# ScalarE takes a second turned map and a second scaling from VectorE in a decoder layer's attention rounds

## What is computed

```python
def masked_softmax(s, mask):
    s = jnp.where(mask, s, NEG_INF)
    e = jnp.where(mask, jnp.exp(s - jnp.max(s, axis=-1, keepdims=True)), 0.0)
    return e / jnp.maximum(jnp.sum(e, axis=-1, keepdims=True), 1e-30)

# differential attention, prompt
p = masked_softmax(s, kpos[None, :] <= qpos[:, None])
a = p[:, :, 0] - lam * p[:, :, 1]
return jnp.einsum('bhqk,bkhv->bqhv', a.astype(v.dtype), v)

# sparse attention: every branch is a masked softmax times its values, then
o_nsa = jnp.sum(o_branches * g_n[..., None], axis=2)
```

## Time and profile before

| | us |
|---|---|
| median of 3 runs | 759.29 (755.44 to 765.13) |
| the profiled execution | 756.94 |
| its span | 755.3 |

### The profile page before, as it was taken

How to read it: one execution, slowest core, us unless ns; L and a number is a source line. 1 busy time by engine, 2 the same in 40 slices (tenths; PEclk the granted TensorE clock), 3 DMA queues, 4 the chain that set the end, 5 groups by cost and what they waited for, 6 DMA issues and landing times.

```text
span 755.3 us, 14050 instructions
## 1 busy us (share of the span) xinstructions
PE 696.8 (92%) x4419; PEld 327.8 (43%) x4419; DVE 488.7 (65%) x976; ACT 205.7 (27%) x530; POOL 105.0 (14%) x198
## 2 busy tenths in 40 slices
PE   6979999999998979999999998968897888999996
PEld 2445545445453535444534643425343352343542
DVE  5366774863865547998597539657769657544373
ACT  3031012112021004322231226524555334333200
POOL 0000000000001001010003556612647100000000
PEclk9999999999999989999999999999999988999999
DMA  8997987998999979999868369978999969985721
GB/s 313 378 330 221 331 263 244 329 368 260 340 379 362 397 261 344 401 320 356 336 209 295 99 194 326 327 243 300 256 318 316 316 205 387 349 268 180 278 114 57
DMA packets 131683, 218.46 MB, mean 289 GB/s; under 512 B 17617, under 2 KB 55738, under 8 KB 130394
## 3 DMA queue, kind: packets, MB, share of 16 engines
q1 hardware_dynamic: 103752, 185.76, 71.6%
q10 hardware_dynamic: 20402, 17.02, 7.3%
q0 software_dynamic: 7456, 14.80, 6.0%
HBM read 211.64 MB, written 10.04 MB: 294 GB/s over the span
## 4 chain that ended last, share of the span: by engine, by line
PE 57%; issue 17%; DVE 8%; DMA 6%; ACTq 4%; POOLq 4%; SPq 2%; POOL 2%; ACT 1%; DVEq 0%
PE banks L690 17%; PE banks L648 9%; PE banks L703 6%; PE banks L1071 4%; ACTq L457 3%; PE banks L789 3%; PE banks L1192 3%; POOLq L476 2%; PE banks L968 2%; DMA ring<-in_dk_cache 1%; PE banks L638 1%; DMA proj<-in_cmp_cache 1%; DMA xn<-in_win_v 1%; POOL ring L480 1%; PE banks L985 1%
## 5 line engine op out<-in xcount | busy, mean ns | idle before, releaser
L690 PE MATMUL banks<-ring,xt 128*128 128x512 f32 (+1 forms) x320 | 130.3, 560 | 0.0
L1445 ACT ACTIVATE wide<-banks,att 128x384 f32<-128x384 f32 (+3 forms) x128 | 66.3, 523 | 121.5 <-DVE att L1947 120.3
L690 PEld LDWEIGHTS banks<-ring,xt 128*128 128x128 f32 x320 | 59.4, 191 | 66.7 <-issue 63.1
L480 POOL DMA_DIRECT2D ring<-in_sel_cache x143 | 75.2, 526 | 45.8 <-issue 40.0
L789 PE MATMUL banks<-ring,small 128*32 128x512 f32 x512 | 70.6, 632 | 2.7 <-DVE xt L1990 2.7
L703 PE MATMUL banks<-ring,small 128*32 128x512 f32 x512 | 62.8, 608 | 3.4 <-DMA ring<-in_dk_cache 3.3
L1946 DVE TENSOR_TENSOR banks<-banks,consts 128x256 f32<-128x256 f32 x64 | 27.4, 428 | 45.9 <-PE banks L968 45.5
L690 PE MATMUL banks<-xt,ring 128*128 128x512 f32 x128 | 56.7, 595 | 0.0
L968 PE MATMUL banks<-proj 64*128 64x384 f32 (+7 forms) x256 | 52.5, 487 | 2.9 <-ACT wide L1445 2.9
L1254 ACT ACTIVATE proj<-banks 128x512 f32<-128x512 f32 (+1 forms) x26 | 14.6, 566 | 147.9 <-PE banks L690 114.7
L1947 DVE TENSOR_REDUCE att<-banks 128x2 f32<-128x768 f32 (+3 forms) x64 | 52.8, 825 | 2.2
(11 more groups left out here) (379 smaller groups left out, 924.4 us busy)
## 6 DMA issues: line engine op xcount, KB each, us to landing
ring<-in_dk_cache SPq DMA_DIRECT2D x256, 256.0 KB, 5.1
ring<-in_dv_cache SPq DMA_DIRECT2D x256, 256.0 KB, 5.2
proj<-in_cmp_cache SPq DMA_DIRECT2D x120, 128.0 KB, 5.4
proj<-in_cmp_cache ACTq DMA_DIRECT2D x104, 128.0 KB, 5.7
ring<-in_w_in SPq DMA_DIRECT2D x6, 2048.0 KB, 13.7
ring<-in_sel_cache POOLq DMA_DIRECT2D x143, 32.0 KB, 5.5
ring<-in_w_out SPq DMA_DIRECT2D x2, 2048.0 KB, 9.3
out_s_win<-in_win_nat SPq DMA_DIRECT2D x1, 4088.0 KB
```

The costliest lines, as they stand in the source:

```text
L480: eng.dma_start(sel_kv[64 * (n % 2):64 * (n % 2) + 64, q % 8, n // 2, :], src["sel_cache"][bass.ds(at, 1), :, :].rearrange("o k n -> (o k) ...
L690: last = mm(banks[:, 3 + n % 2, 0:width(c)], of, by, start=k == 0, stop=k == KC - 1)
L1445: last = A(e_slot(j, c)[:, 0:n], banks[:, 2 * (j % 2) + c, 0:n], ACT.Exp, bias=row_max[:, j % 4, c:c + 1], accum_out=row_sum[:, j % 4, c:c ...
```

## The change

ScalarE's `keep_b0` also copies kind 1 out of bank 5, so it now runs in all four kinds and `keep_b1` on VectorE only in kinds 2 and 3. In the large pair's rounds of kinds 2 and 3 (`by_scalar`) `scale_first` scales both maps, one instruction after the other, and VectorE's L1964 is gone there. In the small pair it stays. No transfer is added or moved. The counts that TensorE waits for follow: bank 5 is free for kind 2 when ScalarE has copied kind 1.

```diff
         def copies_before(j, b):
-            return 3 * (j // 4) + ((0, 1, 1, 2), (0, 0, 1, 2))[b][j % 4]
+            return (4, 2)[b] * (j // 4) + ((0, 1, 2, 3), (0, 0, 0, 1))[b][j % 4]
+        def by_scalar(j):
+            return j % 4 >= 2 and duo(j)[1] == 1
+        def scaled_rounds(j):
+            return sum(not by_scalar(i) for i in range(j + 1))
...
             def turn(j):
                 r, tp, t, kind, n = duo(j)
-                pe.wait_ge(s("scaled"), j + 1)
+                if not by_scalar(j):
+                    pe.wait_ge(s("scaled"), scaled_rounds(j))
...
                     bank = kind if kind < 2 else c
-                    if copies_before(j, bank):
-                        pe.wait_ge(s(f"b{bank}_kept"), copies_before(j, bank))
+                    if kind != 1 and copies_before(j, 0):
+                        pe.wait_ge(s("b0_kept"), copies_before(j, 0) - (1 if kind == 2 and c == 0 else 0))
+                    if bank == 1 and copies_before(j, 1):
+                        pe.wait_ge(s("b1_kept"), copies_before(j, 1))
...
             def values(m):
-                pe.wait_ge(s("b0_kept"), 6 * m + 6)
-                pe.wait_ge(s("b1_kept"), 6 * m + 6)
+                pe.wait_ge(s("b0_kept"), 8 * m + 8)
+                pe.wait_ge(s("b1_kept"), 4 * m + 4)
...
             def scale_first(j):
-                e0 = e_slot(j, 0)[:, 0:n]
-                A(e0, e0, ACT.Copy, scale=row_sum[:, j % 4, 0:1]).then_inc(s("scaled_first"), 1)
+                for c in range(2 if by_scalar(j) else 1):
+                    e = e_slot(j, c)[:, 0:n]
+                    last = A(e, e, ACT.Copy, scale=row_sum[:, j % 4, c:c + 1])
+                last.then_inc(s("scaled_first"), 1)
             def keep_b0(j):
-                to = p_turned_d(0) if kind == 0 else p_turned_n[:, 2 * (kind - 2), :, :]
-                A(to[...], banks[:, 4, 0:n]..., ACT.Copy).then_inc(s("b0_kept"), 1)
+                to = p_turned_d(kind) if kind < 2 else p_turned_n[:, 2 * (kind - 2), :, :]
+                A(to[...], banks[:, 4 + (kind == 1), 0:n]..., ACT.Copy).then_inc(s("b0_kept"), 1)
...
-                if 3 <= j < DUOS + 3 and j % 4 != 0:
+                if 3 <= j < DUOS + 3:
                     keep_b0(j - 3)
...
             def scale(j):
-                    dve.wait_ge(s("weighed"), nsa_rounds(j))
-                    V.tensor_scalar(e1, e1, sums[:, 1:2], None, ALU.mult).then_inc(s("scaled"), 1)
+                    if not by_scalar(j):
+                        dve.wait_ge(s("weighed"), nsa_rounds(j))
+                        V.tensor_scalar(e1, e1, sums[:, 1:2], None, ALU.mult).then_inc(s("scaled"), 1)
             def keep_b1(j):
-                to = p_turned_d(1) if kind == 1 else p_turned_n[:, 2 * (kind - 2) + 1, :, :]
+                to = p_turned_n[:, 2 * (kind - 2) + 1, :, :]
...
-                if 3 <= j < DUOS + 3 and j % 4 != 3:
+                if 3 <= j < DUOS + 3 and (j - 3) % 4 >= 2:
                     keep_b1(j - 3)
```

More of the change, by code:

```diff
@@ L1459, in keep_b0 @@
                 act.wait_ge(s("turned_p"), turns_done(j, 0))
-                to = p_turned_d(0) if kind == 0 else p_turned_n[:, 2 * (kind - 2), :, :]
-                A(to[:, 0:t + 1, P * (t % 2):P * (t % 2) + P], banks[:, 4, 0:n].rearrange("p (k n) -> p k n", n=P),
+                to = p_turned_d(kind) if kind < 2 else p_turned_n[:, 2 * (kind - 2), :, :]
+                A(to[:, 0:t + 1, P * (t % 2):P * (t % 2) + P], banks[:, 4 + (kind == 1), 0:n].rearrange("p (k n) -> p k n", n=P),
                   ACT.Copy).then_inc(s("b0_kept"), 1)
```

## The result

| | before | after |
|---|---|---|
| median, us | 758.26 (752.26 to 765.13, 20 executions) | 760.55 (756.41 to 765.48, 20 executions) |
| profiled execution (span) | 756.94 (755.3) | 761.08 (759.1) |

The ratio is 1.0061, with a 95% interval of 1.0038 to 1.0084: 0.6% slower, and within the 2% that counts as the same. It counts fast executions alone (none over 1.5% above the fastest of its kernel), while the two medians in the table count all and stand at 1.0030. The forecast was 760.9 us, a ratio of 1.0021 to its own base of 759.29.

What follows compares the result with a forecast made beforehand. Bounds took turns: GpSimd's block loads, the selection's ping-pong, those loads again, a mixture, finally TensorE. Terms +0.5 + 0 + 0.35 - 0.2 + 1.0 = +1.65, say +1.6, on 759.29 gave 760.9 us; own range 758.5 to 763, with rivals 755.5 to 766.

Steps and rivals of the forecast that it cites:

- Step 1: Rounds 0 to 12: about 4 us off VectorE come out before a 6.21 us transfer wait at the first gate: 0.0.
- rival C: Waits for ScalarE's copy bite everywhere: 16 turns of kind 2 hold TensorE 0.7 us each, +11, 771 us; chance 0.05.
- Step 2: Rounds 13 to 17, first selection: second scaling and copy on ScalarE delay it, +0.5 us, bounds 0 and +1.2.
- Step 3: Rounds 18 to 36: the stretch still ends with GpSimd's load series, 0.0 us, bounds -0.39 and +1.
- Step 4: Round 41: TensorE's turn of kind 2 waits for ScalarE's copy, delaying value step and second selection, +0.35 us.
- Step 5: Round 44: one copy goes from in front of VectorE's `keep_n(4)`, for which `out_sums(0)` waited 1.54 us: -0.2 us.
- Step 6: Rounds 53 and 61: TensorE waits for ScalarE's copy behind the exponentials, +0.5 us each; bounds for the pair 0 and +1.5.
- rival B: TensorE's clock: earlier arrival and longer idling at both gates bring one to three more half-clock stretches, 762.5 to 766; chance 0.2.
- Rivals A and D: First: GpSimd's series gets shorter, 756.9, chance 0.13. Second: VectorE was the pace, all 14.7 us come out, 744.6, chance 0.03.

Runs made afterwards that it cites:

- the repeat: The changed kernel run once more, unedited, against the kernel before: 759.98 us, ratio 1.0061 (1.0027 to 1.0095).

## Why the prediction was right

The time was right, 760.9 against 760.55, and four of the six steps were; but that the two numbers lie so close is in part luck. The forecast was +1.6 us on a base of 759.29, the median of three executions, and the median of twenty is 758.26. Against that base the change costs 2.3 us by the medians, 3.1 by the means below and 4.6 by the ratio (2.9 to 6.4): the base was 1.0 us too high and the change too low by 0.7 to 3.0, and the two errors cancel. And the largest movement in the trace was foretold with the wrong sign; it did no harm because of the cover beneath it.

*Step 1, rounds 0 to 12: wrong, at a cost of nothing.* The step took the stretch as VectorE's and let 4 us come out of it ahead of the gate. VectorE was not its pace. From the first row maximum to the last ones ahead of the gate its waits were, before and after:

```profile
DVE banks L1946 <- PE banks L968: 5.7, 1, 5.7
```

```profile
DVE banks L1959 <- PE banks L976: 10.1, 6, 6.1
DVE xn L1985 <- PE banks L996: 3.8, 2, 2.1
```

The one wait before is in round 11, for scores that stood behind `values(0)` on TensorE (479.19 to 484.38 us); so VectorE had time to spare there ahead of the gate's own wait. And with the scalings off VectorE and TensorE at full clock throughout, rounds 0 to 12 took 38.83 us (the scalings with the selection's exponential in front), against 38.65 before: what VectorE saved did not come out.

The stretch became 5.35 us longer instead. The windows from round 0 to round 12 of before, of after, and of the kernel with the copy ahead of the exponentials:

```profile
448.78:487.43 38.65, 32.88 (x232) 13.81 (x236) 31.74 (x72) 21.63 (x61) 22.40 (x42) 1.00 1.01 318
```

```profile
450.74:494.74 44.00, 36.09 (x232) 14.34 (x236) 28.99 (x64) 25.00 (x68) 26.02 (x49) 0.92 0.94 289
```

```profile
447.47:488.50 41.03, 35.91 (x232) 14.84 (x236) 28.82 (x65) 25.22 (x69) 23.82 (x45) 0.92 0.97 307
```

Two things add up in it. TensorE was idle for 7.9 us where it had been for 5.8: VectorE used to make the copy of kind 1 while ScalarE made the exponentials, and the new order puts them in series. And it was busy for 3.2 us longer with the same matmuls, since its clock was at half for 6.8 us. In the repeat the shares are 1.2 and 4.5 us, with 10.2 us at half clock. So the waits are the smaller part and the clock the larger.

The waits are rival C, which the prediction priced at 0.7 us for each of 16 turns and set aside for the time. It came true for ten turns, 7.7 us in all, but only 3.4 us of that lie in rounds 0 to 12, where the prediction said that the gate would absorb them. The stretch used up 6 of the 6.21 us of cover: rounds 0 to 14 took 54.64 us before and 54.54 after (54.95 in the repeat, where no wait was left at all). That these three agree is in part luck too. Behind the gate, the way to round 14 took 8.5 and 8.7 us instead of 7.0, for TensorE had less of the work done ahead. But the gate came sooner after round 0, at 46.0 and 46.3 us instead of 47.7: GpSimd issued its last block 41.9 us after round 0 before, 42.9 after and 41.9 in the repeat, and it landed in 5.7, 3.0 and 2.1 us, at a DMA share of 1.01, 0.94 and 0.92. "Depends on no round" holds for GpSimd's issues and not for its landings.

The mistake was to walk row by row through rounds 13 to 17 and 28 to 32 and not through 0 to 4, since "covered" was taken to hold for any sign and size.

*Step 2, rounds 13 to 17: right.* +0.5 was the forecast, +0.48 is measured (18.19 to 18.67), and +0.5 in each kernel with the scalings in front of the selection's exponential. `sel_scale` was to come 0.35 later (the prediction's own terms, 0.61 less 0.3, give 0.31): from the start of the row maximum of round 14 it begins 515.66 - 505.28 = 10.38 us on where it began 10.03 before.

*Step 3, rounds 18 to 36: wrong in its owner, and low.* Zero was the forecast, with bounds of -0.39 and +1. GpSimd's series did not change: its last selected block is issued 66.3 us after `sel_values(0)` (522.6 to 588.9) against 66.2 (520.3 to 586.5):

```profile
586.02 2.85 POOL L488 DMA_DIRECT2D ring<-in_sel_cache  x5 [0.66 <-issue]
```

But VectorE reached the second gate at 596.6 us, after the blocks, and waited for nothing, where a wait of over 1 us had been foretold. The rounds of this stretch became 1.1 and 2.1 us longer, at and over the upper bound of 1. One stretch of 3.4 us at half clock is the difference between the two: it lies in the trace with 2.1 (581.3 to 584.7 us) and not in the other. The kernels with one half of the change show the same. With the scalings the stretch took 69.9 and 70.4 us, each with 3.4 us at half clock, and with the copies 69.1 with none. In the first of those TensorE was busy for 62.4 us against 61.0 before, and idle for 7.5 against 7.9, so its longer time is all clock, and that two scalings in a row cost something of their own does not show. Rounds 18 to 42, with the second gate and round 41 in them, took 92.06 us before and 92.72 and 94.13 after; the kernels with one half of the change lie at 89.7 to 94.6. What of the 1 to 2 us reached the end can't be told from that.

*Step 4, round 41: right.* +0.35 was the forecast, +0.33 is measured (1.20 to 1.53 us, above).

*Step 5, L1038: right.* Its wait went from 1.54 to 1.34 us, the -0.2 of the forecast.

```profile
626.11 0.64 PE L1049 MATMUL banks<-xt,consts 128*32 128x256 f32 x8 [1.34 <-issue]
```

*Step 6, rounds 53 and 61: right.* 0.5 each was the forecast, 0.56 each is measured, in every kernel with the small pair's copies behind the exponentials and in no other (the 7.02 us of the scalings' second trace are the value page). In after, round 53, the place of the earlier trace rows:

```profile
655.25 0.27 ACT L1474 ACTIVATE xt<-banks 128x128 f32<-128x128 f32 x1
655.41 0.41 ACT L1466 ACTIVATE wide<-wide,att 128x128 f32<-128x128 f32 x1
655.58 0.33 PE L996 MATMUL banks<-consts,wide 128*128 128x128 f32 x1 [0.33 <-ACT xt L1474]
655.84 1.06 PE L797 MATMUL banks<-ring,small 128*32 128x512 f32 x8
```

*The engine totals.* VectorE lost 12.4 us where 15 were counted, ScalarE gained 13.2 where 18 were. The groups' durations of the earlier trace rows overlap by the pipeline: the copy above starts at 655.25 and the scaling at 655.41, 0.16 us on, though the copy is given 0.27; two scalings in a row take 1.33 us and not 2 x 0.73. The error was to add durations where start-to-start distances count. Step 2 had used the distance, 0.61, and came out right.

*The clock, rival B: part of the measured difference.* 222 executions have their mean granted clock beside their time (one of 3,903 us left out). Within a kernel, a mean clock lower by 0.01 goes with 5.9 us more. The 86 executions of the kernel before in the experiments have a mean clock of 0.9777 (standard error 0.0004) and the 29 of the changed kernel 0.9752 (0.0010). By that slope 1.5 of the 3.1 us between their mean times (757.5 and 760.6) go with the clock, and 1.6 us (standard error 0.4) remain at the same clock. With the two kernels of the repeat alone, which ran beside each other, 1.7 us remain at the same clock and 2.4 go with the clock. The 1.6 us equal the sum of the steps, but that proves little, for the parts do not add up so. By the same reckoning (standard errors in brackets) the copies alone are at +0.6 us (0.8) where the steps say +1.15, the small pair's copies alone at 0.0 (0.7) where they say +1.15, the scalings alone at -1.7 (0.5) where they say +0.5, and the change without its small-pair part at -1.2 (0.6) where they say +0.5. The steps that the prediction had right are shown in their places in the traces, and not by the total.

Rival B asked for one to three more half-clock stretches; the mean of 1.5 us is about one, its mildest form. By the table over the fourteen traces the copies behind the exponentials bring two or three such stretches into rounds 0 to 12, where there had been none or one, and not behind longer waits at the gates, as rival B had it. That it is the waits of step 1 which make the clock fall is likely and not shown. In after TensorE stood idle for 2.45 us until 464.47 and was at half clock (0.50, that is 1.2 GHz) from 465.3 to 468.7, where the kernel before was at full clock; but the kernel with the copy ahead of the exponentials had no such wait and kept two such stretches, and over all its executions the kernel with the copies alone has a mean clock of 0.9781 (0.0020), like the kernel before. One sign that the prediction named for being wrong did come: the mean clock from 592 to 650 us was to be near 0.85, and it was 0.94 in after. In the repeat it was 0.85.

*Rivals A and D* did not come: GpSimd's series is as long as it was, 66.3 against 66.2 us, although some eight scalings had left VectorE during it, and the time did not fall. The Trainium skill (SBUF — State Buffer, Who interferes with whom) has VectorE's two-port instructions lock GpSimd out. The rows show a little of it, which the earlier trace rows did not. Over the fourteen traces, from 448 to 620 us, the 307 issues of blocks by GpSimd that overlap a scaling on `wide` (L1957 and L1964, and their lines in the other kernels) took 0.556 us on average and the 1343 others 0.533, and all 34 that took over 0.64 us are among the 307. That is 0.02 us each, where rival A had 0.45. In which of its modes VectorE ran a scaling, no row says.

*The value pages.* TensorE waited once for 3.9 us for a page in the rounds after 50 (3.4 in the repeat), which no step had. It comes where the rounds just before ran fast: rounds 42 to 50 took 27.14 us against 29.44, rounds 50 to 63 56.10 against 52.97, and the kernel with copies alone ahead of the exponentials did the same (27.46 and 55.18, a wait of 4.0). Those rounds ran fast by the clock: it was at half for 6.9 us in rounds 42 to 50 before, and for 0 and 3.4 us in these two. So what the clock gives back the page wait takes again: 42 to 63 together are longer by 0.83 and 0.87 us, which is near steps 5 and 6 (+0.9 by their measured sizes).

## What to carry to other kernels

A move of work between engines is judged by where the instruction comes to stand in the new engine's order, and by who waits behind it: walk it through each stretch, those with cover too, since an edit that seems to save in front of a gate can as well spend the whole cover. When a stretch comes out longer, split it into TensorE's busy and idle time before a wait is blamed: of the 5.35 us of rounds 0 to 12, 3.2 were the same matmuls at a lower clock. Put an operation for which TensorE waits in front of the long ones of its round; here the same copy cost TensorE ten waits behind two exponentials, and ahead of them left its list of waits. And add start-to-start distances, not durations, when small instructions follow each other.

## What the hardware showed beyond that

*The price of a half-clock stretch.* Up to round 0 all these kernels do the same work in the same order, and they reach it at 445.96 to 450.96 us. The traces with 3.4 us at half clock in that part (two) reach it at 446.2 on average, those with 6.8 us (six) at 447.7, those with 10.2 us (five) at 450.2, the one with 13.7 us at 450.7. So the second and the third stretch of 3.4 us go with 1.5 and 2.5 us more there, the fourth (one trace) with 0.5, and together they make up most of a scatter that is larger than the whole effect of this change. In rounds 0 to 12, TensorE's busy time for the same matmuls gives the price more directly: 32.7 to 33.2 us without a half-clock stretch (three traces), 34.3 to 34.4 with 3.4 us (four), 35.9 to 36.1 with 6.8 (four) and 37.4 to 37.6 with 10.2 (three), so 1.4 to 1.7 us for each.

*A queue shared with urgent loads.* 39 loads of blocks moved from ScalarE's queue to the one of SyncE that brings the value pages made either kernel 2% slower, more than three times the effect of the change itself: TensorE's waits for pages became 14.6 and 15.2 us. Whether the pages came late because the queue issued the blocks first, or because it waited in order for something that the blocks needed, no run here tells apart.
